# A hybrid diffusion step on one core: the attention phase with TensorE's order, the PSUM ring and the copies dealt anew

## What is computed

```python
def block_attention(q, k, v):
    ...
    def one_block(qi):
        sc = jnp.einsum('bqkgd,btkd->bkgqt', qi, k).astype(jnp.float32) * scale
        pr = jax.nn.softmax(sc, axis=-1).astype(v.dtype)
        return jnp.einsum('bkgqt,btkd->bqkgd', pr, v)

    o = lax.map(one_block, qb)
...
    return (o * jax.nn.silu(g)) @ p['attn_w_out'][j]
```

## Time and profile before

| | |
|---|---|
| median of 3 runs | 4665.88 us |
| lowest, highest | 4664.48, 4666.93 us |
| span of the profiled execution | 4657.5 us |
| attention phase | 1907 to 2435 us |
| one large unit | 7.71 us |
| one small unit | 3.11 us |

### The profile page before, as it was taken

How to read it: one execution, slowest core, us unless ns; L and a number is a source line. 1 busy time by engine, 2 the same in 40 slices (tenths; PEclk the granted TensorE clock), 3 DMA queues, 4 the chain that set the end, 5 groups by cost and what they waited for, 6 DMA issues and landing times. The chain is left out here.

```text
span 4657.5 us, 137485 instructions
## 1 busy us (share of the span) xinstructions
PE 4252.3 (91%) x61184; PEld 3660.8 (79%) x61184; DVE 2695.4 (58%) x4665; ACT 1889.1 (41%) x3496; POOL 4.6 (0%) x10
## 2 busy tenths in 40 slices
PE   6999979999998899999999899889999789999988
PEld 2888868888885799766668899877988678888858
DVE  5433657777775653355556433467425577777755
ACT  5333325555554532355554000155333245555542
POOL 0000000000000000000000000000000000000000
PEclk8999989999999999899999999999999899999999
DMA  7444763333325132100000221112446733323341
GB/s 293 150 125 130 229 220 93 93 86 96 92 76 197 64 79 56 52 1 2 1 6 32 95 95 66 53 59 76 120 127 209 241 109 94 99 85 97 85 184 64
DMA packets 543468, 480.78 MB, mean 103 GB/s; under 512 B 30369, under 2 KB 501665, under 8 KB 535201
## 3 DMA queue, kind: packets, MB, share of 16 engines
q1 hardware_dynamic: 411040, 405.91, 27.7%
q10 hardware_dynamic: 131840, 66.07, 4.9%
HBM read 337.94 MB, written 128.71 MB: 100 GB/s over the span
## 5 line engine op out<-in xcount | busy, mean ns | idle before, releaser
L654 PE MATMUL ps<-big_r,stage_r 128*128 128x384 f32 x2976 | 639.7, 349 | 15.7 <-DVE big_r L916 14.2
L654 PEld LDWEIGHTS ps<-big_r,stage_r 128*128 128x128 f32 x2976 | 522.4, 189 | 70.4 <-issue 25.1
L2531 PE MATMUL ps<-big_r,w_out 128*128 128x384 f32 x2304 | 417.6, 341 | 36.6 <-DVE w_out L2647 36.1
L2531 PEld LDWEIGHTS ps<-big_r,w_out 128*128 128x128 f32 x2304 | 406.7, 191 | 45.7 <-DVE w_out L2647 39.3
L654 PE MATMUL ps<-big_r,w_slab_r 128*128 128x384 f32 x1488 | 341.3, 337 | 0.0
L371 PE MATMUL ps<-big_r,stage_r 128*128 128x384 f32 x1536 | 311.0, 337 | 13.8 <-DVE big_r L358 13.8
L2253 DVE TENSOR_REDUCE extra<-ps 128x1 f32<-128x1152 f32 (+1 forms) x144 | 177.7, 1234 | 205.0 <-PE ps L2158 205.0
L371 PEld LDWEIGHTS ps<-big_r,stage_r 128*128 128x128 f32 x1536 | 269.7, 188 | 29.3 <-issue 26.7
L1510 ACT COPY arena<-ps 128x512 f32<-128x512 f32 x288 | 169.1, 587 | 255.5 <-PE ps L1315 255.2
L654 PEld LDWEIGHTS ps<-big_r,w_slab_r 128*128 128x128 f32 x1488 | 267.9, 189 | 0.0
L1664 DVE COPY_PREDICATED arena<-arena,ps 128x128 f32<-128x128 uint32 x720 | 192.8, 324 | 116.7 <-PE ps L1303 115.8
(11 more groups left out here) (260 smaller groups left out, 8079.7 us busy)
## 6 DMA issues: line engine op xcount, KB each, us to landing
w_slab<-in_w SPq DMA_DIRECT2D x138, 512.0 KB, 3.7
arena<-scan_in SPq DMA_DIRECT2D x144, 320.0 KB, 3.8
arena<-scan_in SPq DMA_DIRECT2D x288, 128.0 KB, 3.8
scan_in<-x_resid ACTq DMA_DIRECT2D x48, 576.0 KB, 4.7
arena<-scan_in SPq DMA_DIRECT2D x48, 576.0 KB, 7.2
arena<-scan_in SPq DMA_DIRECT2D x144, 192.0 KB, 4.0
arena<-in_w_ada SPq DMA_DIRECT2D x24, 1024.0 KB, 5.9
x_resid<-in_w_ada SPq DMA_DIRECT2D x24, 1024.0 KB, 5.1
```

The costliest lines, as they stand in the source:

```text
L654: mm = pe.matmul(g.ps[:, 3 * s + c, 0:CW], w[:, k * P:(k + 1) * P], x[:, k, chunk(c)], start=k == i == 0, stop=k == NB - 1 and i == 2)
L2531: mm = pe.matmul(g.ps[:, bank(i, b), 0:wide[i]], w[:, b, k * P:(k + 1) * P], r, start=k == j == 0, stop=k == NB - 1 and j == 2)
```

## The change

TensorE's order in a unit becomes T00, S of the next unit, T01, T02, V of the unit before, T10, T11, T12 with L; `ring` follows. In the large units, the copies of head 1 that the DVE makes are now groups 0 and 1 instead of 1 and 2; ACT makes group 2, behind the next unit's exponentials, and it waits for `scaled_ok` besides. In the small units, head 1's only copy goes from DVE to ACT. The DVE takes both maxima of the next unit one after the other, then the gate multiplication of the unit before, then its copies, and the scaling is an operation of its own behind them. `values` waits for the ACT copy of the last group and for the DVE copy of the one before it.

```diff
     for n in range(ATT_UNITS):
-        ring += [(n, h, k) for h in range(2) for k in range(attention_groups(n))]
+        ring += [(n, 0, k) for k in range(attention_groups(n))]
         ring += [(n - 1, None, 0)] * (n > 0)
+        ring += [(n, 1, k) for k in range(attention_groups(n))]
...
-    by_vector = lambda n, h, k: last_group(n, h, k) or h == 1 and k == 1
+    by_vector = lambda n, h, k: h == 1 and not last_group(n, h, k)
...
-                elif last_group(n, h, k):
-                    pe.wait_ge(scaled_ok, n + 1)
                 else:
                     pe.wait_ge(tr_vector_ok if by_vector(n, h, k) else tr_ok, copy_count[n, h, k])
+                    if last_group(n, h, k):
+                        pe.wait_ge(scaled_ok, n + 1)
...
-                pe.wait_ge(tr_ok, copy_count[n, 1, 0] if last else copy_count[n, 0, 0])
-                pe.wait_ge(tr_vector_ok, copy_count[n, 1, last])
+                pe.wait_ge(tr_ok, copy_count[n, 1, last])
+                if last:
+                    pe.wait_ge(tr_vector_ok, copy_count[n, 1, last - 1])
...
                 transposes(n, 0, 0)
-                transposes(n, 0, 1)
                 if n + 1 < ATT_UNITS:
                     scores(n + 1)
+                transposes(n, 0, 1)
                 transposes(n, 0, 2)
+                if n:
+                    values(n - 1)
                 transposes(n, 1, 0)
                 transposes(n, 1, 1)
                 transposes(n, 1, 2)
-                if n:
-                    values(n - 1)
...
+                if last_group(n, h, k):
+                    act.wait_ge(scaled_ok, n + 1)
...
-                for h, k in ((0, 0), (0, 1), (0, 2), (1, 0)):
-                    turned(n, h, k)
+                for k in range(3):
+                    turned(n, 0, k)
                 if n + 1 < ATT_UNITS:
                     exps(n + 1, 0)
                     exps(n + 1, 1)
+                turned(n, 1, attention_groups(n) - 1)
...
-                if last_group(n, 1, k):
-                    V.tensor_tensor(gate_of(n), g.ps[:, bank_of(n, 1, k), 3 * P:4 * P], gate_of(n), op=ALU.mult).then_inc(scaled_ok, 1)
+
+            def scaled(n):
+                k = attention_groups(n) - 1
+                dve.wait_ge(tr_mm, group(n, 1, k) + 1)
+                V.tensor_tensor(gate_of(n), g.ps[:, bank_of(n, 1, k), 3 * P:4 * P], gate_of(n), op=ALU.mult).then_inc(scaled_ok, 1)
...
                 if n + 1 < ATT_UNITS:
                     maximum(n + 1, 0)
+                    maximum(n + 1, 1)
+                if n:
+                    gated(n - 1)
                 turned(n, 0)
                 turned(n, 1)
-                if n + 1 < ATT_UNITS:
-                    maximum(n + 1, 1)
-                turned(n, 2)
-                if n:
-                    gated(n - 1)
+                scaled(n)
```

## The result

The changed kernel takes 4682.69 us in the median of 5 runs (4675.06 to 4691.48), the kernel before 4665.38 us in the median of 5 (4660.20 to 4666.93). The ratio is 1.0038, with a 95% interval of 1.0027 to 1.0050: slower by about 17 us. Both intervals hold the ratio of the sum, 1.0043.

A forecast was written before the change was run, and what follows sets the result against it. TensorE, waiting on the two-bank PSUM ring, was taken to bound attention. Large units +20.5, last unit +1.9 and small units -2.5 gave +19.9 us on 4665.88: 4685.8 us, range 4673 to 4696.

The forecast's parts named there:

- The walk: Large attention unit followed step by step from T00: 8.04 us against 7.71, plus 0.33; time 4676 to 4694, chance 0.83.
- L to T00: Step from the inverse-row-sum matmuls to the next unit's first transposes: taken as 0.37 us, bounds 0.26 and 0.40.
- The copies' turn: Transpose group, over its copy, to the group taking its bank: 1.17 us with a scalar copy, 1.25 with a vector copy.
- both new waits: In a large unit, V waits 0.37 us for T01's bank and T12 0.41 us for T10's bank.
- Maxima together is worth nothing: Large units: the score loop gets 0.8 us shorter but has 1.6 us of slack, so no gain.
- The last unit: End of attention, without scores for cover: 8.1 us before, last gate ending at 10.0 after, plus 1.9 us.
- The term for the small units: Start of attention: the 0.44 us wait for an exponential before scores goes; at most 3 us, taken as -2.5 us.
- a sign of a wrong walk: The walk is wrong if the stretch from small units to the first large one moves by more than 5 us.
- The ring that does not bind: Rival: V, T11 and T12 go without waiting, large unit 7.06 us, about 4625 us; chance 0.06.
- the gaps between kinds: Rival: these TensorE gaps shrink after bank waits, and L to T00 costs 0.26 or less; 4674 us, chance 0.09.
- The clock did not fall: Rival: TensorE's clock falls; a tenth of the units at the lower clock gives +40 us, 4730 us; chance 0.02.
- 8.4 us lie outside the span: Whole kernel: median 4665.88 us against a profiled span of 4657.5; the difference was carried over unchanged.

The follow-up runs named there:

- e5: The changed kernel with T01's scalar copy cut to one of three blocks in the large units; ratio 1.0021 against the kernel before.
- e6: The changed kernel with T10's vector copy cut to one of three blocks in the large units; ratio 1.0012 against the kernel before.
- e9: The changed kernel with both T01's scalar copy and T10's vector copy cut to one of three blocks; ratio 0.9978 against the kernel before.
- e4: The changed kernel with head 0's exponential made once more in each large unit; 4682.83 us against 4659.05 for the kernel before.
- e1: The kernel before with only both maxima of the next unit taken together, ahead of the vector copies; 4714.28 us against 4659.05.
- e10: The changed kernel, unaltered, timed again in a second session; 4672.39 us against 4649.91 for the kernel before.
- e2: The kernel before with only the next unit's scores moved ahead of T01; 4667.67 us against 4659.05.
- e8: The kernel before with maxima together, T11's copy on the scalar engine, and the scores' 128-column pair between T10 and T11; 4635.83 us against 4655.07.
- e3: The changed kernel with the scores put back behind T01; 4697.16 us against 4659.05 for the kernel before.

## Why the prediction was right

**The walk.** Each step of it stands in the timeline of the changed kernel: scores 0.48 behind T00, V at 3.79, T11 at 6.46, T12 at 7.20 for 7.19, L at 7.68 for 7.67, the unit at 8.04. T12's late copy starts at 0.49 for 0.4 and is covered by S, as forecast. The one number that had never been seen, L to T00, was taken as 0.37 from a load and a gap, and is 0.36 to 0.37. 62 x 0.33 is the main term, 20.5. From the scores of the third large unit to T00 of the last one the time grew by 21.3 us. Of the 0.8 us more, 0.5 is a slip in the sum: it counts units from scores to scores, but the last one from T00, and T00 now stands 0.48 ahead of the next scores, where it stood 0.99.

**The copies' turn.** That both new waits end with a copy of the ring, and in one chain, was argued from the timeline of before and is shown by e5, e6 and e9, which shorten nothing but the copies.

**"Maxima together is worth nothing".** The score loop does have the slack that the prediction gave it: e4 makes it 1.25 us longer, and the full units stay at 8.05. The changed kernel with its maxima apart was not run. As the price of that part alone, put into the kernel before, "nothing" would have been wrong by 55 us (e1). The prediction said which copy had stood between the maxima, but did not say that V hung on it. It could be left out only because the copies had moved too.

**The last unit.** +1.9 us was forecast and 1.9 measured (10.0 against 8.1), by the steps that were named: T01 at 1.0, the last V at 7.5 for 7.4, the gate's end at 10.0.

**The start of the phase.** The term for the small units was too small. From the first scores to the first large scores the time fell by 3.4 us (24.0 to 20.5), and in e10 by 2.8, for the 2.5 that were taken and the 3 that were called the most. The later ones gained 0.3 to 0.4 us each, where 2.5 for seven makes 0.36, but the second gained 1.4 us, and 0.9 in e10, where its scores ran at the lower clock as before. The two large units behind them, which the sum left out, gave 0.8 us more (17.3 to 16.5). The prediction let a clock that rises earlier into its range, not into its sum. Over the whole start the phase got 4.3 us shorter, short of the 5 us that were named as a sign of a wrong walk. So the phase changed by +18.9 (21.3, 1.9 and -4.3) for the +19.9 that were summed, and part of the closeness is that the start and the large units erred in opposite ways.

**The other side.** The ring that does not bind (7.06 a unit) did not come: the turn is 1.17 and 1.26. Nor did the gaps between kinds shrink behind a wait: L stands 0.48 behind T12, as it did before. The clock did not fall: it was granted at 1.00 in the 501 us, with three waits of 0.2 to 0.4 us a unit. The Trainium skill reports in "TensorE: Matmul & The Clock Gate", section "A second HAM failure mode: psum-queue depth-cycling", a kernel whose clock swings as short idles between its groups recur. That was not seen here.

**What was wrong.** The sentence that 8.4 us lie outside the span set the median of other runs against the span of one. The changed kernel's runs each lie 1.8 us above their own span (4682.81 and 4681.0). It cancelled, as both terms were carried over. The parts of the program outside attention scatter by about that much. Behind the last gate multiplication it ran 2223.4 us in the profiled run before and 2231.4 in that after, while the profiled runs of the experiments lie between 2224 and 2234 with the same code there. The changed kernel itself was profiled twice: 2231.4 and 2228.6 us behind the phase, and 1904.0 and 1893.6 us ahead of its first scores. What causes this stays open. So it is in part luck that the median of 4682.7 lies only 3 us from the 4685.8 of the forecast. The two sessions give +17 and +22, and it is the phase in the trace, 18.9, that tests the walk.

## What to carry over

When a few PSUM banks are used in turn, walk the order of uses. Ask of each what emptied the bank before it, and what stands between. Here a bare turn is 1.2 us and a group of three transposes 0.32. So where two pairs of groups follow each other, the second pair waits unless about half a microsecond of other work lies between (T10 in e2). Work put inside the ring that needs the bank just filled waits too (V in the changed kernel). Cutting a piece off the scores and placing it where a pair waits (e8) was what gained most. A stall that the profile shows is not the price of an edit that removes it: the ring hands it to the next use (e3), and an engine's queue hands it to whoever waits for the copy behind (e1).

## What the runs showed of the hardware

- The releaser named in a row can be off on the weight loads: in the changed kernel T12's load is put down to an exponential, its matmul to the vector copy, and shortening the copy (e6) moved T12 from 0.74 to 0.48 us behind T11 while the exponential kept its place.
- The transposes come later behind a scores matmul of 512 columns than behind one of 128: in e8 the two pairs of 512 columns take 1.92 us from their first load to the transposes, where 1.71 was worked out as the whole 2.14 less the small pair's 0.43.
- At a granted clock of 1.00 and without a longer wait, the weight loads stand idle for 0.17 us from transposes to V (e3), to L or to scores, and from V or L to transposes (the changed kernel). None is shown from scores that end with the 128-column pair to transposes, nor from L to V.
- The same code outside the changed phase differed by up to 11 us between profiled executions (2223.4 to 2234.3 us behind the phase), more than half of the effect measured here.
